# Padding tiles that shift the FFN weight ring, the projection slices and the mixing weights in on-chip memory

## The reference, cut to what matters

```python
# end of the mixer of block one, then the query projection of the experts
return (g_attn * y_attn + g_sgu * y_sgu) @ w_out      # y_attn = o @ w_branch_attn
q = rmsnorm((xt @ w_query).reshape(T, PEER_HEADS, 2, PEER_PK_DIM))
# twice in block two: a projection by w_o, then the feed-forward layer (D_FF = 2816)
h = ... @ w_o
x = layer_norm(DN_ALPHA * x + h, ...)
u = x @ w_up                                          # 1024 -> 5632
u = sum(up[:, j:j + S] * conv_w[j] for j in range(CONV_W)) + conv_b
gate, val = jnp.split(u, 2, axis=-1)
f = (jax.nn.silu(gate) * val) @ w_down                # 2816 -> 1024
```

## Time and profile before

| | |
|---|---|
| median of three runs | 3725.96 us |
| span of the profiled execution, first to last instruction | 3713.8 us |
| the rest of the median (12.2 us) | lies around the span |
| TensorE matmul busy | 3528.9 us, 95% of the span |
| TensorE weight load busy | 2862.4 us, 77% |
| VectorE, ScalarE, GpSimd busy | 62%, 40%, 36% |
| mean granted TensorE clock | 0.962 |

### The profile page before, as it was taken

One profiled execution on the slowest core, in us unless ns is written; L12 is line 12 of the kernel. 1 busy time (PEld: TensorE's weight loads), 2 busy tenths in 40 slices (PEclk: granted clock), 3 DMA queues, 4 the chain that ended last, 5 costly groups with the idle time before them and its releaser, 6 DMA issues. The chain is left out here.

```text
span 3713.8 us, 58353 instructions
## 1 busy us (share of the span) xinstructions
PE 3528.9 (95%) x22109; PEld 2862.4 (77%) x22109; DVE 2290.8 (62%) x3622; ACT 1476.7 (40%) x2438; POOL 1341.5 (36%) x821
## 2 busy tenths in 40 slices
PE   8999988899998999899999899998999998989998
PEld 4777866788988999788888444897888864678887
DVE  5723167425999887688888866445566236646642
ACT  3312246334546996233333233223255214424540
POOL 3723400434776334454222011430334521413352
PEclk9999999999999999999999999999999997699999
DMA  7633410635678989999999335213333331032331
GB/s 273 228 101 113 168 48 1 238 128 168 220 224 274 323 318 342 361 369 364 357 349 360 105 115 169 80 32 119 90 100 91 113 132 69 1 115 81 100 113 57
DMA packets 367108, 651.14 MB, mean 175 GB/s; under 512 B 23944, under 2 KB 227592, under 8 KB 363716
## 3 DMA queue, kind: packets, MB, share of 16 engines
q1 hardware_dynamic: 321468, 475.37, 38.7%
q0 software_dynamic: 36864, 134.23, 9.7%
q10 hardware_dynamic: 8584, 38.89, 2.7%
HBM read 557.64 MB, written 96.00 MB: 176 GB/s over the span
## 5 line engine op out<-in xcount | busy, mean ns | idle before, releaser
L100 PE MATMUL ex_hb<-wb_x_hi,ex_uh 128*128 128x384 f32 x1024 | 350.8, 343 | 17.5 <-POOL ex_ul L1684 11.3
L101 PE MATMUL ex_hb<-wb_x_lo,ex_uh 128*128 128x384 f32 x1024 | 344.7, 337 | 0.0
L102 PE MATMUL ex_hb<-wb_x_hi,ex_ul 128*128 128x384 f32 x1024 | 344.5, 336 | 0.0
L100 PE MATMUL es_ob<-es_vh,es_ah 128*128 128x512 f32 x768 | 300.2, 391 | 11.8 <-DVE es_al L2056 11.8
L100 PE MATMUL pf_acc<-wb_x_hi,pf_wh 128*128 128x512 f32 (+2 forms) x768 | 298.3, 388 | 7.0 <-DVE wb_x_lo L2484 4.7
L101 PE MATMUL es_ob<-es_vl,es_ah 128*128 128x512 f32 x768 | 299.8, 390 | 0.0
L102 PE MATMUL es_ob<-es_vh,es_al 128*128 128x512 f32 x768 | 299.7, 390 | 0.0
L101 PE MATMUL pf_acc<-wb_x_lo,pf_wh 128*128 128x512 f32 (+2 forms) x768 | 297.7, 388 | 0.0
L102 PE MATMUL pf_acc<-wb_x_hi,pf_wl 128*128 128x512 f32 (+2 forms) x768 | 297.5, 387 | 0.0
L2035 POOL DMA_INDIRECT es_near<-in_peer_v,wb_picked x128 | 178.4, 1394 | 325.9 <-DVE wb_po L2059 320.6
L728 POOL TENSOR_TENSOR ip_wl<-ip_raw,ip_wh 128x512 fp32r<-128x512 f32 x128 | 190.8, 1499 | 226.8 <-ACT ip_wh L652 226.6
(11 more groups left out here) (536 smaller groups left out, 8889.1 us busy)
## 6 DMA issues: line engine op xcount, KB each, us to landing
ex_u<-in_uT SPq DMA_DIRECT2D x128, 512.0 KB, 4.8
es_v<-in_peer_v SPq DMA_DIRECT2D x31, 2048.0 KB, 17.2
ip_raw<-in_w_in SPq DMA_DIRECT2D x112, 256.0 KB, 4.2
scratch_act<-ex_ge SPq DMA_DIRECT2D x128, 192.0 KB, 4.9
scratch_G<-eg_gates ACTq DMA_DIRECT2D x12, 2048.0 KB, 9.2
es_ge<-scratch_act SPq DMA_DIRECT2D x31, 768.0 KB, 6.2
es_g<-scratch_G SPq DMA_DIRECT2D x31, 768.0 KB, 10.1
fo_raw<-in_w_up SPq DMA_DIRECT2D x44, 512.0 KB, 5.3
```

Of the source, the lines that this page charges most:

```text
L100: pe.matmul(out, left[0], right[0], start=start, stop=False)
L101: pe.matmul(out, left[0], right[1], start=False, stop=False)
L102: return pe.matmul(out, left[1], right[0], start=False, stop=stop)
```

## The change

Two new tiles that nothing reads or writes are declared, and two skipped stretches are made longer. No instruction is added, removed or put in another order; only addresses differ.

```diff
@@ the phase of the mixing weights
         raw = sb("mq_raw", [P, 2, D])
+        shim = sb("mq_shim", [P, 104])
         with ExitStack() as own:
             ah = sb("mq_ah", [P, KD, D], F32R)
@@ first_slices
-        hold = sb(f"{name}_hold_a", [P, 18400])
+        hold = sb(f"{name}_hold_a", [P, 18432])
         pl = sb(f"{name}_pl", [P, KD, D], F32R)
-        hold = sb(f"{name}_hold_b", [P, 2520])
+        hold = sb(f"{name}_hold_b", [P, 2560])
         ph = sb(f"{name}_ph", [P, KD, D], F32R)
@@ projected_ffn
         raw, ph, pl, first_loaded, SPLIT = first
+        shim = sb("pf_shim", [P, 72])
         wh = sb("pf_wh", [P, 2, 2, D], F32R)
```

## The result

| | before | after |
|---|---|---|
| median of 6 runs each | 3719.51 us | 3699.43 us |
| lowest to highest | 3716.55 to 3726.20 | 3694.03 to 3704.09 |
| span of the profiled execution | 3713.8 us | 3698.2 us |

The ratio is 0.9944 with a 95% interval of 0.9933 to 0.9954: faster by 20 us, 17 to 25 by the interval. The forecast was a gain of 23 us and a time of 3703.

What follows compares the result with a forecast made beforehand. Touched stretches were taken as bound by matmul count times start distance. Gains of 5.1, 1.7, 12.9, 0.6 and 3.2 us made 23.5, less 0.5: 23 us, from 3726.0 to about 3703, range 3692 to 3715.

Steps and rivals of the forecast that it cites:

- The views: Busy times, TensorE's waits and timeline: touched stretches last matmul count times start distance, 226.7 ns where operand residues modulo 512 agree.
- The addresses: Moved tiles of mixing, w_o slices, weight ring and hidden tiles all land at residue 128 modulo 512, order unchanged.
- The sum: Gains over mixing, query, w_o, up and down projections: together 23.5 us, taken as 23 us after 0.5 off.
- wide pieces: 384-column matmuls in the up projection's first two chunks: 192 at 3.4 ns, 0.6 us gained.
- the own slots: Down-projection matmuls with moving weights in pf_wh/pf_wl: 3 x 192, at 226.8 ns already, no gain.
- w_o projections: Projections by w_o in both calls: 384 matmuls gain 4.4 ns each, 1.7 us.
- Span and median: Whole kernel: span falls from 3713.8 to 3690.8 us; median lies 12.2 above it, from 3726.0 to about 3703.
- Rival 2: 128-column pieces after the handoff wait: clock may flip in either call; both half 3713, both full 3693, chance 0.13 each.
- Rival 4: Up loop gains only half of what the down loop does: 6.5 us missing, 3710; chance 0.05.
- Rival 1: Address isn't the cause or tiles land elsewhere; time stays at 3726; chance 0.06.
- What has to keep up: Up loop: GpSimd's pf_wl split stays ahead of TensorE, margin shrinking by 0.32 us from 4.20 to 3.9.
- Rival 3: GpSimd's pf_wl split sets the up loop's pace, giving 24 us back (3727) or running slower; chance 0.03.

Runs made afterwards that it cites:

- e3: Kernel before with only the 416-byte mq_shim added in the mixing phase; 3713.11 us.
- e5: Kernel before with only the 288-byte pf_shim added before the weight ring, hold_c at 3184; 3703.57 us, ratio 0.9955.
- e1: Kernel after, with the last token tile's transposes moved ahead of the last 384-column up-projection group in both feed-forward calls; median 3681.38 us, ratio to before 0.9902.
- e2: Kernel before, with the last token tile's transposes moved ahead of the last 384-column up-projection group, addresses unchanged; median 3703.82 us, ratio to before 0.9957.
- e8: Kernel after with the weight ring at -128 bytes (first call) and 256 (second) against the moving tile, mixing tiles at 256; 3705.05 us.
- e9: Kernel after with the early transposes and every moved tile at residue 384 modulo 512; median 3682.11 us, ratio to before 0.9897.
- e7: Kernel after with the weight ring at -32 bytes (first call) and -64 (second) against the moving tile, mixing tiles at +32; 3718.59 us.
- e10: Kernel after with the weight ring at +64 bytes (first call) and +128 (second) against the moving tile, mixing tiles at +128; 3722.22 us.

## Why the prediction was right, point by point

- **The views.** That the stretches are bound by the distance between starts, and that this distance hangs on the two addresses, was right; e3 to e5 show it part by part. The rule was too narrow: equality modulo 512 is sufficient, but modulo 256 is enough. The rows of before could not tell the two apart, since none of them has tiles 256 bytes apart.
- **The addresses** are as worked out, and the spacings answered to them in every stage. GpSimd's split takes 4607 ns by its median after, where it took 4609 to 4622.
- **The sum.** 23 us, against 22.4 us with the handoffs covered (e1, e2) and 20.1 (17 to 25) for the change itself. Terms, from the stretches: mixing and query 5.3 (5.1 predicted), the up loops 6.3 and 6.6 (12.9), wide pieces 0.3 in each call (0.6), down 1.8 + 1.8 (3.2; the own slots, put at nothing, went from 227.4 to 226.7 ns in the mean of all their intervals, 0.4 us). Together with the w_o projections that is 22.9. Those gave 0.4 and 0.0 where 0.85 each was due. Their spacing is right (226.7 ns), and two things took the gain back. The 16 transposes in the midst of the stage, which wait for VectorE's rows, took 2.25 us where they had taken 1.91 (second call 2.13 and 2.00): TensorE now comes to them sooner. And in the second call three more matmuls of the stage stood 427 ns apart, at the lower clock, 0.6 us.
- **Span and median.** One step failed: I put the 12.2 us between span and median "around the span". The runs with a span on record show 2.0 to 2.1 us around it (3700.20 against 3698.2). The profiled execution of before was a quick one, about 3715.8 us in its own time by that measure; the rest is scatter between runs. So the span after was not 3690.8 but 3698.2, a fall of 15.65 us and not of 23. The base was wrong too: 3726 was the high end of before, whose median over six runs is 3719.5. That put the forecast 6.5 us too high, and a gain 2.9 us larger than the one measured took part of it back. That 3703 came within 3.6 us of 3699.4 is in this part luck. The chance of a faster kernel, by the terms named, adds up to 0.86 and not 0.84.
- **Rival 2** came about in the profile: the handoff of the first call fell to half clock. I gave that 0.13, having seen it stay up once. In the ten profiles with the handoff uncovered the pieces of the first call took 33.5 us twice and 38 to 41 us eight times, and those of the second call 38 to 41 us all ten times. The quick case of the earlier trace rows was the rarer one. The change did not lose 7 us by it in the medians; that most of its runs and most of those of before alike had the slow case is the likely reason, and with one profile of each it is not shown.
- **Rival 4** did not come: the up loops gained the full 6.6 to 6.7 ns a matmul.
- **Rival 1** is refuted by e3 to e5 and e8: moving a tile and nothing else changes the spacing by 6.6 ns in just its own stage. The rule of the Trainium skill beside it (page "TensorE: Matmul & The Clock Gate", section "Step-by-step: what each phase is for": the next weight load takes no read bandwidth from the running matmul) doesn't foresee this; the measurement decides.
- **What has to keep up.** The margin of GpSimd's split before TensorE was to shrink by 0.32 us, from 4.20 to 3.9. It shrank by 0.30 us, from 3.50 to 3.20. The loss was right; the margin was misread. TensorE waits for the split at the head of a half turn, and the matmul that I took in the earlier trace rows is the fourth of its half turn. The heads are these, before and then after:

```profile
2761.75 0.40 PE L100 MATMUL pf_acc<-wb_x_hi,pf_wh 128*128 128x512 f32 x1
```

```profile
2753.83 4.61 POOL L2439 TENSOR_TENSOR pf_wl<-fo_raw,pf_wh 128x2048 fp32r<-128x2048 f32 x1 [6.27 <-ACT pf_wh L2370]
...
2761.64 0.39 PE L100 MATMUL pf_acc<-wb_x_hi,pf_wh 128*128 128x512 f32 x1
```

That is 2761.75 - 2758.25 and 2761.64 - 2758.44. Rival 3 did not come. The waits of ScalarE for TensorE's results in this loop shrank by as much. The shorter of the two, before and then after:

```profile
2750.95 0.78 ACT L2391 ACTIVATE pf_cv<-pf_acc,pf_cb,pf_cw 128x512 f32<-128x512 f32 x1 [0.51 <-PE pf_acc L102]
```

```profile
2751.17 0.78 ACT L2393 ACTIVATE pf_cv<-pf_acc,pf_cb,pf_cw 128x512 f32<-128x512 f32 x1 [0.21 <-PE pf_acc L102]
```

With 0.21 us left against 3.20 for the split, a much faster TensorE in this loop would find the chain through ScalarE first. That is an argument from these rows, and no run tried it.

## What to carry to other kernels

Read the distance between starts of dense matmuls, shape by shape, and compare places where the same shape differs only in its tiles; 6.6 ns in 227 is invisible in busy shares (95% before and after) and was worth 22 us over 3552 matmuls here. Lay out the two operand tiles of such products so that their addresses agree modulo 256 bytes; skipped tiles of 32 and 160 bytes were enough in e9. Before pricing a change of this size, look at every short wait of TensorE in front of light work. Behind one of 2.4 us, with 8 transposes before it, the narrow matmuls took up to 10 us more at the lower clock, and issuing the transposes earlier in both calls brought 16 to 18 us.

## What the runs showed of the hardware that was not expected

- The spacing of dense float32r matmuls depends on the relative address of their stationary and moving tiles: 226.7 ns at 0 or 256 bytes, 229.0 at -64, 232.4 at +128, 233.3 at +64, -32 and -128 with the stationary tile shifted, and 233.3 at +32 with the moving one (e7 to e10), all for 512 columns at full clock. For 384 columns agreement brought 3 ns, 176.6 to 173.6 (first to last of 96, before and after). For 128 columns it brought nothing: 111.1 ns in e1 and in e2.
- The same wait of 2.37 us, at the same place in the program, left the mean granted clock of the stretch around it at 0.99 in the profile of before and at 0.75 in that of after.
